# Final RMSNorm rows of the first four token tiles: scaling moved from VectorE to ScalarE, gain multiply moved to GpSimd

## What is computed

```python
def rms_norm(x, g):
    y = x * lax.rsqrt(jnp.mean(x * x, axis=-1, keepdims=True) + RMS_EPS)
    return y * g

def swiglu(h, w_ffn_in_l, w_ffn_out_l):
    gu = h @ w_ffn_in_l
    return (jax.nn.silu(gu[..., :D_FF]) * gu[..., D_FF:]) @ w_ffn_out_l

hp = hp + swiglu(rms_norm(hp, g_ffn[l]), w_ffn_in[l], w_ffn_out[l])
...
y_prompt, y_sample = rms_norm(hp, g_final), rms_norm(hs, g_final)
```

## Time and profile before

| what | value |
|---|---|
| median of 3 runs | 2037.14 us (2036.2 to 2041.29) |
| the profiled execution: its own time | 2039.44 us |
| its span, first to last instruction | 2037.6 us |
| mean granted TensorE clock | 0.978 of full speed |
| busy share PE, DVE, ACT, POOL | 94%, 67%, 35%, 40% |

### The profile page before, as it was taken

One profiled execution on the slowest core, in us unless ns is written; L12 is line 12 of the kernel. 1 busy time (PEld: TensorE's weight loads), 2 busy tenths in 40 slices (PEclk: granted clock), 3 DMA queues, 4 the chain that ended last, 5 costly groups with the idle time before them and its releaser, 6 DMA issues. The chain is left out here.

```text
span 2037.6 us, 35844 instructions
## 1 busy us (share of the span) xinstructions
PE 1918.8 (94%) x13605; PEld 1742.8 (86%) x13605; DVE 1360.1 (67%) x2491; ACT 712.6 (35%) x1456; POOL 815.7 (40%) x848
## 2 busy tenths in 40 slices
PE   6889999999999898998799989899999999999997
PEld 6867788899997697555489987899999999999997
DVE  5037999996988164544456233778777888875675
ACT  5234322222222374344332234752322323243433
POOL 4757766578892042455300210304223453410020
PEclk9999999999999999999899999999999999999999
DMA  5122223236764642220376102057767787687544
GB/s 173 33 66 75 75 86 100 95 124 202 254 204 138 233 151 80 58 63 9 114 208 168 42 23 83 11 187 247 242 205 258 256 285 239 214 282 236 175 139 143
DMA packets 235695, 304.35 MB, mean 149 GB/s; under 512 B 31812, under 2 KB 188260, under 8 KB 234884
## 3 DMA queue, kind: packets, MB, share of 16 engines
q1 hardware_dynamic: 206452, 232.38, 36.2%
q0 software_dynamic: 6032, 43.06, 6.0%
q10 hardware_dynamic: 23040, 26.63, 3.7%
HBM read 228.18 MB, written 101.15 MB: 162 GB/s over the span
## 5 line engine op out<-in xcount | busy, mean ns | idle before, releaser
L1122 PE MATMUL pz<-w_hi,n_hi 128*128 128x384 f32 (+2 forms) x656 | 226.1, 345 | 3.8 <-DVE n_lo L909 3.4
L1122 PE MATMUL pz<-w_hi,n_lo 128*128 128x384 f32 (+2 forms) x656 | 219.8, 335 | 0.0
L1122 PE MATMUL pz<-w_lo,n_hi 128*128 128x384 f32 (+2 forms) x656 | 219.5, 335 | 0.0
L966 DVE MATCH_REPLACE8 sel<-m,sel 128x1024 f32<-128x1024 f32 (+4 forms) x224 | 206.1, 928 | 0.0
L963 DVE MAX8 m<-sel 128x8 f32<-128x1024 f32 (+4 forms) x224 | 198.2, 931 | 0.1
L4129 PE MATMUL p_c<-n_t_hi,blk 128*128 128x264 f32 x1120 | 191.3, 285 | 1.3 <-DVE blk L3807 1.3
L4129 PEld LDWEIGHTS p_c<-n_t_hi,blk 128*128 128x128 f32 x1120 | 159.0, 188 | 1.5 <-issue 1.5
L1122 PEld LDWEIGHTS pz<-w_hi,n_hi 128*128 128x128 f32 x656 | 127.2, 194 | 24.4 <-issue 18.8
L4129 PE MATMUL p_c<-mix_hi,blk 128*128 128x264 f32 x816 | 141.2, 285 | 0.2 <-issue 0.2
L823 POOL TENSOR_TENSOR rot<-z,rope 128x384 f32<-128x384 f32 (+3 forms) x90 | 75.2, 835 | 140.9 <-ACT z L624 134.6
L1128 PE MATMUL pz<-n_hi,w_hi 128*128 128x352 f32 x384 | 126.2, 329 | 2.9 <-ACT z L614 2.5
(11 more groups left out here) (541 smaller groups left out, 5223.4 us busy)
## 6 DMA issues: line engine op xcount, KB each, us to landing
shared<-in_w_in SPq DMA_DIRECT2D x26, 768.0 KB, 4.6
blk_raw<-in_w_ffn_in SPq DMA_DIRECT2D x72, 256.0 KB, 3.7
relu<-z_qb SPq DMA_DIRECT2D x24, 512.0 KB, 5.1
t_s<-h_t SPq DMA_DIRECT2D x44, 264.0 KB, 6.0
h_t<-in_w_ffn_out SPq DMA_DIRECT2D x44, 256.0 KB
s_w<-h_t SPq DMA_DIRECT2D x44, 256.0 KB, 3.4
z_b<-z ACTq DMA_DIRECT2D x48, 192.0 KB, 1.9
gates<-z ACTq DMA_DIRECT2D x48, 176.0 KB, 3.2
```

The lines of the kernel that those rows point to most:

```text
L966: dve.match_replace(out=sel[0:r, o:o + n], in_to_replace=m8[0:r, u, :], in_values=sel[0:r, o:o + n], imm_value=PICKED).then_inc(s_rep, 1)
L1122: m = pe.matmul(out, tokens(a, k, i), b[:, n % 2, k, 0:w], start=(k == 0 and p == 0), stop=(k == KC - 1 and p == 2))
```

## The change

For tiles 0 to 3, VectorE's `norm` ends after the reciprocal. ScalarE waits for that reciprocal, for tile 3 also for the store of the row buffer's earlier row, and copies the bank to the row buffer with the reciprocal as the per-partition scale. GpSimd multiplies the row buffer by `g_final` in place. The row's store waits for GpSimd, and the next `turn` waits for ScalarE's copy (`s_scaled`). Tiles 4 to 8 stay as they were.

```diff
+SCALED = 4
...
                 def store(i):
                     r0, r = i * P, norm_rows_of(i)
-                    sp.wait_ge(s_n, i + 1)
+                    sp.wait_ge(*((s_gained, i + 1) if i < SCALED else (s_n, i + 1 - SCALED)))
...
                         pool.tensor_tensor(h, h, sum_of(c), ALU.add).then_inc(s_hp, 1)
+                for i in range(SCALED):
+                    pool.wait_ge(s_scaled, i + 1)
+                    if i == 0:
+                        pool.wait_ge(s_const, 16)
+                    pool.tensor_tensor(norm_row(i % 3), norm_row(i % 3), norm_row(3), ALU.mult).then_inc(s_gained, 1)
                 pool.wait_ge(s_win, 16 * 3 * DB)
...
                     act.activation(stat[0:r, i, 2:3], stat[0:r, i, 0:1], ACT.Sqrt, scale=1.0 / D, bias=eps[0:r, :]).then_inc(s_root, 1)
+                    if i < SCALED:
+                        act.wait_ge(s_inv, i + 1)
+                        if i >= 3:
+                            act.wait_ge(s_out[i % 3], 16 * (i // 3))
+                        act.activation(norm_row(i % 3), turned(i)[:, :, :], ACT.Copy, scale=stat[:, i, 3:4]).then_inc(s_scaled, 1)
...
                     dve.reciprocal(stat[0:r, i, 3:4], stat[0:r, i, 2:3]).then_inc(s_inv, 1)
+                    if i < SCALED:
+                        return
                     dve.wait_ge(s_inv, i + 1)
-                    if i == 0:
+                    if i == SCALED:
                         dve.wait_ge(s_const, 16)
...
                     if 1 <= i < 6:
-                        pe.wait_ge(s_n, i)
+                        pe.wait_ge(*((s_scaled, i) if i <= SCALED else (s_n, i - SCALED)))
```

More of the change, by code:

```diff
@@ L3393, in feed_forward @@
         s_t, s_sq, s_eps, s_root, s_inv, s_n = sem("g_t"), sem("g_sq"), sem("g_eps"), sem("g_root"), sem("g_inv"), sem("g_n")
+        s_scaled, s_gained = sem("g_scaled"), sem("g_gained")
         s_out = [sem(f"g_row{u}") for u in range(3)]
```

## The result

Over 20 runs of each kernel the changed one takes 2046.88 us and the one before 2041.66 us (medians). The medians lie 5.2 us apart; the ratio estimated from all runs is 1.0023, with a 95% interval of 1.0013 to 1.0033, which is slower by 4.7 us, between 2.7 and 6.7. That is inside the 0.3% called no change, but on the slower side beyond its interval, and 1.8 times the forecast of 2.6. The measured time lies above the stated range of 2036.4 to 2042.6. Two things moved it: the median of the kernel before is itself 4.5 us above the three-run median from which the forecast started, and a term was too small. The starting point alone would have been enough (2041.66 + 2.6 = 2044.3); the term alone would not have left the range of times (2037.14 + 4.5 = 2041.6), though it is above the bound of +3.4 on the change.

The account below looks back on a forecast made before the run. TensorE was taken to bound the kernel, with VectorE counting only where TensorE waits. Tile 4's turn moves 1.5 + 1.1 = +2.6 us, so 2037.14 + 2.6 = 2039.7 us; range 2036.4 to 2042.6.

Parts of the forecast that it names:

- The starting point: Median of the runs of the kernel before, 2037.14 us, to which the forecast added its 2.6 us.
- bound of +3.4: Upper bound on the delay of tile 4's turn and the end: 1.9 + 1.5 us, by the 1.81 us row.
- What bounds: TensorE is busy 94% of the span; VectorE counts only where TensorE waits, 2.0 us before chunks 79 and 81.
- tile 0: Copy and multiply fall where TensorE works on chunks made earlier; nothing on the path.
- tile 2: ScalarE waits for reciprocal 2 with high parts of chunks 83 to 85 queued behind; costed at nothing.
- queues: Stores of rows 1 and 2 and the loads behind them move later; both hidden, by over 2 us.
- ScalarE's order: At tile 1 the copy stands ahead of chunk 79's high part; VectorE's 1.2 us saved become 0.4 us lost.
- One sign: In the changed trace, ScalarE would wait 3 us for reciprocal 2 (L3972) near 2008.
- GpSimd beside VectorE: GpSimd's multiply slows VectorE's two-SBUF-input low parts of chunks 79 and 80 from 0.6 to 1.15 us each.
- Rival (c): TensorE's clock falls in a grown gap before chunk 79 or 81: +6.9 us, 2044.0 us; chance 0.03.
- A clock that drops before 2026: Sign that the prediction is wrong: the clock column of the changed trace drops before 2026.
- Rival (b): VectorE's relief reaches TensorE: chunk 81 0.9 us earlier, tile 4's turn another 1.0, 2035.2 us; chance 0.12.

Follow-up runs that it names:

- e1_no_gain: Changed kernel without GpSimd's four multiplies by g_final; from tile 0's turn to tile 4's 27.48 us, against 31.04 changed and 26.53 before.
- e2_quarters: Changed kernel with each GpSimd multiply split into four of 128x256; from tile 0's turn to tile 4's 29.37 us, against 31.04 changed and 26.53 before.
- w1_order: Kernel before with only VectorE's order changed (rows of tiles 1 and 3, end of pass 12 later); tile 0's turn to tile 4's 24.52 us, against 26.53.
- e3_late_copy: Changed kernel without GpSimd's multiplies, ScalarE's copies of tiles 1 and 3 moved behind the next high parts; tile 0's turn to tile 4's 24.84 us, before 26.53.

## Why the prediction was right or wrong

**What bounds, tile 0, tile 2, queues: right in what they cost.** Tile 0 cost 0.01 and tile 2 nothing. For tile 2 the reason given was not right: its first low part was to come 1.4 us before TensorE wanted it, and it came late, so that TensorE waited 0.48 us at chunk 83. That cost nothing because the chain went over VectorE and ScalarE beside it. The stores that waited longer delayed nothing. From tile 4's turn to the end it is 18.36 us against 18.66, where the forecast had no change.

**ScalarE's order: right, and in size.** Forecast 0.4 at each of tiles 1 and 3; e1_no_gain has 0.95 for both. The copy costs 1.11 us, not the 1.03 of the square.

**One sign did not come out.** ScalarE was to stand 3 us for reciprocal 2; it stood 0.33 us, because tile 2's turn itself came 3.4 us late (16.34 us after tile 0's instead of 12.97), behind the delayed and slowed chunk 79. In e1_no_gain and e2_quarters, where the clock held there, it stood 1.90 and 2.44 us.

**GpSimd beside VectorE: the mechanism in part, the size wrong.** This is the step that failed. The prediction took the rows 1.81 and 2.41 as a rate, a low part that runs at half speed beside GpSimd, and charged 1.1 us at tile 1 and 0.7 at tile 3. Measured is 1.76 at each (2.44 - 0.68, and 2.45 - 0.69). It could have been read from the earlier trace rows: the low part of 1.81 us began at 1593.34 and ended at 1595.15, and GpSimd's instruction ended at 1594.61, 0.54 us before. That 0.54 is the same in the changed kernel and in the quarters. The L3717 rows that looked cheaper were cheaper because GpSimd's instructions there are 264 wide and take 0.82 to 1.22 us each (16 of them before); the lock lasts as long as one instruction of the other side, and the new one takes 2.38. The Trainium skill, SBUF — State Buffer, section "Who interferes with whom", states this: the port pair that the two engines share is an exclusive lock, whoever comes second is blocked and not slowed, and a VectorE instruction with at most one SBUF input stays out of it. The runs agree on both (2.44 against 0.68; 1.28 unchanged beside 2.37). The prediction used a page that says only that the two contend.

With the measured term the sum is 2 x (0.45 + 1.76) = 4.4, against 4.51. The upper bound of +3.4 was no bound: it took the longest row seen, not the longest wait that a 2.38 us instruction can make.

**Rival (c), the clock: wrong in its condition, and in its effect.** The prediction wanted a gap near 3.3 us; the clock fell after 2.45, 2.44 and 2.42 us, and not after gaps of 1.80 in e2_quarters or 1.26 in e1_no_gain. The length of a gap doesn't decide it alone: all ten profiles have a gap of 1.99 us before the turns of tiles 6 to 8, and the clock fell right behind it in e2_quarters and w1_order and in none of the other eight. A clock that drops before 2026 was one of the prediction's own signs of being wrong, and it came. But the fall lay beside VectorE's own delay and reached the end with some 0.1 us. It took 1.56 us of TensorE's time (3.92 - 2.36), and at full clock TensorE would have been through chunk 80 by 2007.6, with 1.5 us to stand until chunk 81. The prediction had worked out that wait of TensorE for VectorE itself, but did not set it against the rival.

**Rival (b), relief: wrong here for the reason given**, and e3_late_copy shows that it is worth 1.69 us once the copy is out of the way.

**The starting point.** Three runs gave 2037.14, twenty gave 2041.66. The range allowed 2.0 up for that, while one of the three runs was 4.2 higher. That the forecast started low was bad luck with three runs, not a mechanism; the profiles show the scatter to arise before tile 0's turn.

## What to carry to other kernels

Work given to GpSimd is priced by what it does to VectorE: in these runs each VectorE instruction with two SBUF inputs that came up while a GpSimd multiply or add of SBUF tensors ran waited for that instruction's end. So put long GpSimd instructions where VectorE reads banks or idles; cutting them up takes off only a part (4.51 us became 2.84), since more instructions are hit. Relief of an engine counts only if nothing new stands ahead of what that engine waits for: here one copy in front of one rounding turned 1.2 us saved into 0.45 lost. When a contended row is the only evidence, compare its end with the other engine's end before calling it a rate.

## What the runs showed of the hardware that was not expected

The lock works both ways: two GpSimd quarters took 1.18 us each beside VectorE's low parts, where the first and last took 0.73 and 0.72, while the whole multiply, which came first, took its lone 2.36. TensorE's granted clock went to the 1.2 GHz level after single gaps of 2.45, 2.44 and 2.42 us in otherwise full work, and stayed up after 1.80; after the same gap of 1.99 us near the end it fell in two profiles and stayed up in the other eight. ScalarE's copy of 128x1024 out of a bank with a per-partition scale took 1.11 us, against 1.03 for the square of the same bank.
